# A two-block transformer forward pass: the order of the tensor engine's queue in the recurrent tiles is changed

## The reference, cut to what matters

```python
def rwkv7_step(state, inp):
    r_t, w_t, k_t, v_t, kk_t, a_t = inp
    sa = jnp.einsum('bhvk,bhk->bhv', state, -kk_t)
    state = (state * w_t[:, :, None, :] + sa[..., None] * (kk_t * a_t)[:, :, None, :]
             + v_t[..., None] * k_t[:, :, None, :])
    y = jnp.einsum('bhvk,bhk->bhv', state, r_t)
    return state, y
...
    y = (y - mean) * lax.rsqrt(var + GN_EPS)          # over each head
    y = y * gn_w + gn_b
    y = y + jnp.sum(rh * kh * r_k, axis=-1, keepdims=True) * vh      # the "bonus"
...
    mix = jnp.concatenate([o_nsa, o_rwkv], axis=-1)
    return x + mix @ w_out                            # then a final RMS norm of the rows
```

## Time and profile before

| | |
|---|---|
| median of 3 runs | 1299.01 us |
| the profiled execution's own time | 1299.44 us |
| span from its first to its last instruction | 1297.7 us |
| PE busy (matmul) | 1178.4 us, 91% of the span |
| DVE busy | 642.5 us, 50% |
| ACT busy | 508.3 us, 39% |
| POOL busy | 414.7 us, 32% |
| recurrence, from its first product to the end | 1092.45 us to 1297.7 us |

### The profile page before, as it was taken

How to read it: one execution, slowest core, us unless ns; L and a number is a source line. 1 busy time by engine, 2 the same in 40 slices (tenths; PEclk the granted TensorE clock), 3 DMA queues, 4 the chain that set the end, 5 groups by cost and what they waited for, 6 DMA issues and landing times.

```text
span 1297.7 us, 25153 instructions
## 1 busy us (share of the span) xinstructions
PE 1178.4 (91%) x10613; PEld 991.7 (76%) x10613; DVE 642.5 (50%) x1362; ACT 508.3 (39%) x982; POOL 414.7 (32%) x214
## 2 busy tenths in 40 slices
PE   3999997989798999899997959998999899799996
PEld 3988885879798998666797949976777777587763
DVE  5000012971737349888426484116863666245547
ACT  4322224651324332688523262243863421132221
POOL 4644455844524344200344325222004450000000
PEclk9999998999999999999998979997999999899999
DMA  7433332312112222200221221441002312100001
GB/s 201 137 96 97 97 114 85 80 52 68 64 66 66 77 87 97 65 1 2 85 80 61 71 97 49 131 136 43 2 2 69 94 65 89 55 8 3 3 3 65
DMA packets 73177, 89.61 MB, mean 69 GB/s; under 512 B 1993, under 2 KB 66634, under 8 KB 72938
## 3 DMA queue, kind: packets, MB, share of 16 engines
q1 hardware_dynamic: 70136, 78.65, 18.8%
q0 software_dynamic: 2416, 8.26, 2.4%
q10 hardware_dynamic: 514, 1.11, 0.3%
HBM read 83.75 MB, written 4.26 MB: 68 GB/s over the span
## 4 chain that ended last, share of the span: by engine, by line
PE 58%; DVE 11%; issue 7%; ACT 4%; POOL 2%; DMA 1%; DVEq 0%; ACTq 0%; POOLq 0%
PE bank L469 53%; PE bank L726 2%; DMA x<-x_kept 1%; PE bank L891 1%; DVE stat L1763 1%; DVE hT L1871 1%; DVE x L1912 1%; ACT arena L1266 1%; POOL ring_parts L2468 1%; ACT ring_parts L1295 1%; PE bank L647 1%; DVE stat L1764 1%; POOL arena L2585 1%; DVE arena L1786 1%; DVE arena L1774 1%
## 5 line engine op out<-in xcount | busy, mean ns | idle before, releaser
L2468 POOL TENSOR_TENSOR ring_parts<-ring,ring_parts 128x2048 fp32r<-128x2048 f32 (+1 forms) x59 | 269.1, 4561 | 390.5 <-ACT ring_parts L1295 390.2
L469 PE MATMUL bank<-ring_parts,hT_parts 128*128 128x256 f32 x1664 | 334.2, 287 | 19.0 <-DVE arena_parts L1797 10.9
L469 PE MATMUL bank<-hT_parts,ring_parts 128*128 128x512 f32 x896 | 288.5, 400 | 10.3 <-POOL ring_parts L2468 4.9
L469 PEld LDWEIGHTS bank<-ring_parts,hT_parts 128*128 128x128 f32 x1664 | 273.0, 195 | 20.8 <-issue 11.2
L1266 ACT ACTIVATE arena<-bank 128x512 f32<-128x512 f32 (+4 forms) x363 | 170.5, 530 | 278.1 <-PE bank L469 271.1
L469 PE MATMUL bank<-ring_parts,arena_parts 128*128 128x256 f32 x1088 | 260.1, 288 | 7.5 <-POOL hT_parts L2485 7.5
L469 PE MATMUL bank<-arena 64*64 64x64 f32 (+8 forms) x3472 | 223.7, 278 | 19.0 <-DVE stat L1860 7.1
L469 PEld LDWEIGHTS bank<-arena 64*64 64x64 f32 (+3 forms) x3472 | 163.7, 144 | 68.6 <-ACT arena L1266 18.9
L469 PEld LDWEIGHTS bank<-hT_parts,ring_parts 128*128 128x128 f32 x896 | 172.2, 192 | 53.6 <-issue 7.2
L469 PEld LDWEIGHTS bank<-ring_parts,arena_parts 128*128 128x128 f32 x1088 | 192.9, 194 | 8.5 <-POOL hT_parts L2485 8.1
L1295 ACT ACTIVATE ring_parts<-ring 128x2048 fp32r<-128x2048 f32 (+1 forms) x59 | 111.0, 1884 | 78.6 <-PE bank L469 78.6
(11 more groups left out here) (234 smaller groups left out, 1476.3 us busy)
## 6 DMA issues: line engine op xcount, KB each, us to landing
ring<-in_a_w_in SPq DMA_DIRECT2D x16, 1024.0 KB, 5.4
ring<-in_w_in SPq DMA_DIRECT2D x15, 1024.0 KB, 5.6
ring<-in_b_w_in SPq DMA_DIRECT2D x10, 1024.0 KB, 5.0
ring<-in_ple_w_gate SPq DMA_DIRECT2D x8, 1024.0 KB, 5.1
arena<-rpb_rows POOLq DMA_DIRECT2D x16, 256.0 KB, 3.4
ring<-in_a_w_out SPq DMA_DIRECT2D x4, 1024.0 KB, 5.1
ring<-in_b_w_out SPq DMA_DIRECT2D x4, 1024.0 KB, 5.2
ring<-in_w_out SPq DMA_DIRECT2D x4, 1024.0 KB, 5.2
```

The costliest lines, as they stand in the source:

```text
L469: return nc.tensor.matmul(o, l, r, start=start, stop=stop)
L2468: nc.gpsimd.tensor_tensor(rounded(r), r, read_back(high_slot(n)[:, 0:m]), ALU.subtract)\
```

## The change

- In tile 0, `token_major(0)` is issued before the first projection instead of behind it. Of that projection three matmuls follow it, and the fourth is issued behind the last bonus product. VectorE adds it to x after the four multiplications by the bonus products, not before them.
- In the loop over tiles, `grams(i)` is issued before `solved(i - 1)` instead of behind it.
- In the loop, the fourth piece of the late projection is no longer issued between RR and the spread job. There is one behind the square job, and the pieces move up one place, so that the last stands right before RR. VectorE's `add_half(*late)` moves from behind the `plus` of RR to before it.
- GpSimd waits for all four row tiles of x before it issues the DMA of the final gain row.

```diff
--- before.py
+++ after.py
@@ -1158,8 +1158,8 @@
                 end(ins)
 
             grams(0)
-            out_part(0, 0, 0)
             token_major(0)
+            out_part(0, 0, 0, 3)
             pe.wait_ge(S("R_bx"), 1)
             spread("bb", 0)
             values(0)
@@ -1169,6 +1169,7 @@
             product(("D2", 0), "a", mA, mD)
             spread("bb", 2)
             spread("bb", 3)
+            out_part(0, 0, 0, 1)
             pe.wait_ge(S("R_q1"), 1)
             product(("Q2", 0), "v", mD2, Qa, ("D2",))
             product(("D4", 0), "a", mA2, mD2)
@@ -1192,8 +1193,8 @@
             for i in range(1, NT):
                 p = i - 1
                 early, late = beside[i]
+                grams(i)
                 solved(p)
-                grams(i)
                 out_part(*early)
                 state_maps(p)
                 state_adds(p)
@@ -1217,6 +1218,7 @@
                 out_part(*late, 1)
                 turned(i)
                 square_job(p)
+                out_part(*late, 1)
                 product(("KT", i), "a", mE, mA2, ("QT",))
                 product(("K", i), "a", mA2, mE)
                 out_part(*late, 1)
@@ -1224,7 +1226,6 @@
                 product(("K2", i), "a", mA, mD)
                 out_part(*late, 1)
                 product(("RR", i), "v", mD2, Qa, ("Q5", "K2"))
-                out_part(*late, 1)
                 spread_job(p)
 
             p = NT - 1
@@ -2390,12 +2391,12 @@
                 STT(x[:, i, :], x[:, i, :], y, gb2[:, :], ALU.mult, ALU.mult).then_inc(S("out_ready"), 1)
 
             masks(0)
-            add_half(0, 0, 0)
             dve.wait_ge(S("R_mix"), 13)
             for j in range(4):
                 key = ("bb", j)
                 b = take(dve, key)
                 give(TT(rF[:, j, :], vF[:, j, :], b[:, :], ALU.mult), key)
+            add_half(0, 0, 0)
             dve.wait_ge(S("R_q1"), 1)
             plus(("Q2", 0), Qb, Qa)
             plus(("Q3", 0), Qa, Qb, ("Q2", 0))
@@ -2421,8 +2422,8 @@
                 plus(("Q4", i), Qb, Qa, ("Q3", i))
                 spread_of(p)
                 plus(("Q5", i), Qa, Qb, ("Q4", i))
+                add_half(*late)
                 plus(("RR", i), mT, Qa, ("Q5", i))
-                add_half(*late)
                 finish(p)
                 gate(p)
                 bonus(i)
@@ -2586,6 +2587,8 @@
                     .then_inc(S("R_dif"), 1)
             lower(HI[("Rg", 1)])
             pool.wait_ge(S("R_ar"), 16)
+            for i in range(NT):
+                pool.wait_ge(s_x[i], 32)
             pool.dma_start(gb2[:, :], bass.AP(A["final_g_2"].tensor, 0, [[0, P], [1, D]])).then_inc(s_gb[1], 16)
```

## The result

The changed kernel took 1284.94 us, the median of 4 runs (1284.17 to 1287.45), against 1298.97 us for the kernel before beside it (4 runs, 1294.62 to 1300.76). The ratio is 0.9912, with a 95% interval of 0.9889 to 0.9935. The profiled execution took 1287.45 us, its span 1285.6; before, 1299.44 and 1297.7.

What follows compares the result with a forecast made beforehand. PE was taken as the bound, with only its gaps and clock to win back; 4.9 us in tile 0 (6.4 less 1.5 for the clock) plus 2.7 in the loop made 7.6 us, giving 1291.4 us, range 1288.3 to 1294.3.

Steps and rivals of the forecast that it cites:

- The sign: Whole kernel: faster, by more than the 2.6 us a measurement can tell from no change, at a chance of 0.94.
- At 2.9 us I take it as lost: New PE gap before Q2: the clock drops to half for 3.4 us of small products, costing 1.5 us.
- The clock stays up: Rival at the 2.9 us gap before Q2: no clock loss there, 1289.9 us; chance 0.25.
- The x term: Start of tile 0: reordering gains 5.16 us; deferring the gain row lands x 1.24 us earlier; 6.4 us together before the clock.
- The loop: Loop over tiles: late-piece and grams reordering remove PE gaps, gaining 2.7 us, from 1.9 to 3.4.
- The new wait at the early projection: Steps 2 and 3: the early projection waits about 0.15 us for the first gram bank, freed by the first mask pair.
- The end: Last step, no grams behind it: solved(3) waits for the plus of RR, giving back about 0.4 us.
- The anchor: Starting time the gain was subtracted from: median 1299.01 us of the kernel before, 0.4 below the profiled execution.
- x did come earlier: Against the rival that x does not come earlier: Q2 at 1110.49, total 1293.2 us; chance 0.10.
- the margins: Rival at the spread jobs and early projection: margins too small, 0.5 us lost in three steps, 1292.9 us; chance 0.08.
- the masks: Rival in the loop: PE waits for the last mask, 3.8 us in each of three steps, 1302.8 us; chance 0.03.
- The list of PE's gaps behind VectorE: Last 240 us: five PE gaps released by VectorE: 6.6 us before A2, three of 0.9, one of 0.8.

Runs made afterwards that it cites:

- the hold: The changed kernel, with GpSimd also waiting for VectorE's R_kx before lowering the weights of R 4: 1284.93 us, ratio 0.9903; measured again 1283.34 us, ratio 0.9907.

## Why the prediction was wrong

**The sign and the mechanisms held.** A2 no longer waits; the stall sits before Q2 with the addition as its releaser; the gaps at the spread jobs and the first solving product are gone.

**The step that failed is the clock.** "At 2.9 us I take it as lost": it was not lost, at any gap of 1.94 to 3.33 us in this place, over seven traced executions (the changed kernel three times, with the hold twice, and tile 0's moves with and without the later gain row). It was lost at 4.67 us before Q2, and at 5.10 and 6.4 to 6.6 before A2. The 1.5 us were therefore not paid. My error was to carry gaps over from another stage, from one trace, as if length alone decided. The three gaps of the earlier trace rows come again in all 18 traced executions, and the code there is the same in all. The one of 2.12 us never brought the clock down. The one of 2.25 us did in 16 of the 18 and the one of 3.2 us in 16 of the 18; the two exceptions of each are not the same traces. Here is the 2.25 us gap in a second execution of the kernel before, with the clock kept, where the earlier trace rows have 0.76:

```profile
338.06 0.47 PE L469 MATMUL bank<-ring_parts,hT_parts 128*128 128x256 f32 x2 [2.25 <-POOL arena_parts L2474]
```

```profile
337.00:344.00 7.00, 5.94 (x51) 5.97 (x52) 6.36 (x24) 2.67 (x6) 5.15 (x4) 1.00 0.45 152
```

So even the same gap in the same kernel can go either way. Nor does the clock fall in the gap itself there. In the trace PE goes on at 339.20, with the clock still at 1.00 for the next microsecond:

```profile
339.20:340.20 1.00, 0.99 (x8) 1.00 (x9) 0.88 (x4) 0.61 (x2) 1.00 (x1) 1.00 1.09 383
340.20:341.20 1.00, 1.00 (x8) 1.00 (x7) 0.93 (x3) 0.62 (x2) 0.94 (x2) 0.60 1.09 386
```

In the last stage the longest gap without a fall, 3.33 us, is one execution; the other six lie at 1.94 to 2.48. Four of the seven were longer than 2.25 us and none lost the clock, so the place matters too; what else decides is not shown by these runs. "The clock stays up" was a rival at 0.25 with 1289.9 us.

**The x term was nearly right.** Forecast to Q2 before the clock 6.4. Measured 6.7 and 7.1 against the first trace, and 6.5 between the means of the five traces with the old start (22.48 to 23.20 us) and the six with the new start and the later gain row (16.11 to 16.66). One gain row costs x 1.34 us when added and 0.9 to 1.5 when taken away, from pair to pair of traces, against 1.24. PE's own work ended where I had put it, 14.2 against 13.9 us after the gram product.

**The loop was sized 1.0 us too small** (2.7 against 3.7). The new wait at the early projection fits the forecast 0.15 us, though the trace prints no gap: spread job to early projection took 4.73 us before and takes 4.85. VectorE's side of the turn, which answers to the earlier trace rows:

```profile
1162.91 0.69 DVE L2295 TENSOR_TENSOR x<-x,bank 128x512 f32<-128x512 f32 x1 [1.29 <-PE bank L469]
1164.00 0.69 DVE L2285 TENSOR_TENSOR arena<-bank,arena 128x512 f32<-128x512 f32 x1 [0.40 <-PE bank L469]
1164.61 0.68 DVE L2322 TENSOR_TENSOR arena<-arena,bank 128x512 f32<-128x512 f32 x1
...
1167.10 0.68 DVE L2333 TENSOR_TENSOR arena<-arena,vec 128x512 f32<-128x512 f32 x1
...
1168.04 0.55 DVE L2349 TENSOR_TENSOR ring<-bank,cst 128x384 f32<-128x384 f32 x1
```

The addition ends as RR does, the `plus` follows, the bonus is at 1167.10, the first mask pair ends at 1168.59 and the projection is issued at 1168.73. But I had summed the gaps as the trace prints them. A gap is counted from the modelled end of the last matmul, which overlaps the start of the next by 0.07. By start times each spread-job gap was 0.94 (1210.40 + 1.06 to 1212.40), and a whole step went from 38.09 to 37.15: 0.94 net, where I had 0.72. From RR of tile 0 to the first spread job it went from 39.47 to 37.43, 2.0 instead of the 1.7 forecast (0.8 and 0.87). The end gave back 0.2 instead of 0.4. About 0.1 us a step more came from the second piece behind the square job, which now also covers ScalarE's copy before KT (from the start of QT to KT 2.06 us before, and 1.06 for a piece elsewhere; now 3.03 with the piece between).

**The anchor was off too, and the range ignored it.** The forecast gain of 7.6 us, with 1.5 for the clock, 1.0 for the loop and 0.3 for x, makes the 10.4 us of the trace. The medians differ by 14.0, 11.9 and 13.3. The kernel before, over 69 runs on several chips, has a mean of 1297.0; the changed kernel over 16 runs 1285.45. That is 11.5 us, 10.2 to 10.8 of it in the traced recurrence; where the rest comes from is open (the collision ahead may be a part). I had taken the first three runs (1298.92 to 1300.76) for the spread, widening by 0.3 us; the true one is 1291 to 1303, and 1299.01 lay 2 us over its middle. With the 10.4 us known exactly, 1299.0 less 10.4 is still 1288.6, 3.7 us over the result, and the mean of the 16 runs still lies 2.9 us below the range.

**Rivals.** x did come earlier; the margins were not eaten; the masks did not become the bound. The list of PE's gaps behind VectorE left out one of 1.8 us before the last spread job; it is 1.77 us before and 1.78 after, so nothing hangs on it.

## What to carry to other kernels

When an in-order engine stops for a bank, ask whose bank it is: a product that never reads x stood 6.6 us for x because the rotation gave it that bank, and moving the slow reader four products later won most of it. Sum removed gaps by the start times of what stands around them, not by the printed idle time. And before naming a range, look for what makes executions of the same code differ; here one collision moves the time by 3 to 4 us, as much as the range's half-width of 3.0, and a clock that fell in one trace need not fall in the next.

## What the runs showed of the hardware

- A read-back whose source had 2 as its outermost dimension used two of 16 DMA engines, 53 GB/s; with 64 it moved 210 to 240 GB/s at a share of 0.93 or more.
- A broadcast of 512 KB in another queue delayed the two-engine read-back by 0.9 to 1.5 us each, and the one on all engines by nothing that reached PE.
- In the last stage PE's clock stayed at 2.4 GHz over idle gaps of 1.94 to 3.33 us (seven traces) and fell to 1.2 at 4.67 us and more (seven traces). Elsewhere one gap of 2.25 us and one of 3.2 us each brought it down in 16 of 18 traces, and one of 2.12 us in none.
- A VectorE instruction on 128x32 elements with two SBUF inputs took 4.57 us beside GpSimd's 4.58 us; the same line took 0.19 in the same execution before GpSimd began.
